# A four-layer pooling and linear-attention trunk: output projection one block later, first attention blocks recorded inside the last pooling unit, loads of x from another queue

## The reference, cut to what matters

```python
h = concat(meta, x)                                  # (8, 16 + 2048, 1024)
for i in range(4):
    j = i // 2
    if i % 2 == 0: h = h + pool_mixer(rmsnorm(h, pool_norm[j]), ...)
    else:          h = h + gla_mixer(rmsnorm(h, gla_norm[j]), ...)
return rmsnorm(h, final_norm)[:, 16:]

def pool_mixer(h, w_in, w_grp, scale, w_out):
    u, z = split(h @ w_in, 2)                        # 2048 channels each, 4 groups of 512
    t[g] = trailing_mean(u[g], window=(2, 4, 8, 16)[g]) - u[g]
    y = einsum(t, w_grp) * scale * silu(z)
    return y @ w_out

def gla_mixer(h, w_in, w_gate2, b_gate, head_norm, w_out):
    q, k, v, z, glr = split(h @ w_in)                # 4 heads, dk 256, dv 512, gate rank 16
    log_a = log_sigmoid(glr @ w_gate2 + b_gate) / 16
    # chunk by chunk: decayed q and k, masked attention within the chunk, carried state S
    o = per_head_rmsnorm(att @ v + qe @ S) * head_norm
    return (o * silu(z)) @ w_out
```

## Time and profile before

| What | Value |
|---|---|
| Median of 3 runs | 1991.08 us (1990.86 to 2058.15) |
| Profiled execution | 2008.14 us; span of its slowest core (3) 2006.5 us |
| Spans of its eight cores | 1978.1 to 2006.5 us |
| PE (TensorE matmul) busy on core 3 | 1907.1 us, 95% of the span |
| VectorE, ScalarE, POOL busy | 66%, 64%, 22% |
| DMA moved | 106.99 MB, mean 53 GB/s |
| Chain that ended last | PE 79%, DVE 5%, issue 5%, POOL 4%, DMA 4%, ACT 3% |

### The profile page before, as it was taken

How to read it: one execution, slowest core, us unless ns; L and a number is a source line. 1 busy time by engine, 2 the same in 40 slices (tenths; PEclk the granted TensorE clock), 3 DMA queues, 4 the chain that set the end, 5 groups by cost and what they waited for, 6 DMA issues and landing times.

```text
span 2006.5 us, 45600 instructions; the slowest of 8 cores (1978.1 to 2006.5 us)
## 1 busy us (share of the span) xinstructions
PE 1907.1 (95%) x16072; PEld 1357.0 (68%) x16072; DVE 1323.1 (66%) x2159; ACT 1293.4 (64%) x2727; POOL 447.6 (22%) x469
## 2 busy tenths in 40 slices
PE   3999999989999999999999999998899999999997
PEld 2767667755666776777676766776667777776774
DVE  1845565765667777777775556467667777777787
ACT  4855445655567666677885545555666766766786
POOL 1747753210000000000015768331100000000000
PEclk8999999987899999999999999999899999999999
DMA  9431212442121212113333212233512212121112
GB/s 186 100 61 33 43 33 43 78 76 59 29 50 30 51 30 45 38 28 58 61 66 60 44 33 36 40 58 74 93 33 38 43 30 51 30 51 31 41 66 83
DMA packets 105152, 106.99 MB, mean 53 GB/s; under 512 B 90192, under 2 KB 92128, under 8 KB 97888
## 3 DMA queue, kind: packets, MB, share of 16 engines
q0 software_dynamic: 11472, 63.53, 18.0%
q1 hardware_dynamic: 91152, 32.17, 7.4%
q10 hardware_dynamic: 2304, 8.39, 1.5%
HBM read 138.22 MB, written 8.39 MB: 73 GB/s over the span
## 4 chain that ended last, share of the span: by engine, by line
PE 79%; DVE 5%; issue 5%; POOL 4%; DMA 4%; ACT 3%; ACTq 0%; DVEq 0%; SPq 0%; POOLq 0%
PE ps L407 79%; DMA hnT<-hnb 3%; POOL SA L446 2%; POOL SB L446 2%; DVE Y L446 1%; DVE hnb L441 1%; DMA gbc<-gains 1%; DMA h<-x 1%; ACT hnb L435 1%; DVE Eq L780 0%; ACT Eq L435 0%; POOL U L451 0%; DVE h L446 0%; ACT sg L435 0%; DVE S L441 0%
## 5 line engine op out<-in xcount | busy, mean ns | idle before, releaser
L407 PE MATMUL ps<-hnT,W 128*128 128x256 bf16 (+1 forms) x9216 | 984.1, 264 | 9.5 <-DVE qe L441 3.6
L407 PEld LDWEIGHTS ps<-hnT,W 128*128 128x128 bf16 x9216 | 832.9, 99 | 155.5 <-issue 19.6
L441 DVE SCALAR_TENSOR_TENSOR h<-ps,rs,h 128x512 f32<-128x512 f32 x256 | 191.4, 748 | 155.5 <-ACT rs L435 130.1
L407 PE MATMUL ps<-W,Y 128*128 128x512 bf16 x1024 | 250.8, 387 | 16.9 <-DVE Y L446 15.1
L407 PE MATMUL ps<-W,hnT 128*128 128x512 bf16 x1088 | 261.7, 385 | 0.0
L446 DVE TENSOR_TENSOR h<-h,ps 128x512 f32<-128x512 f32 x256 | 175.1, 685 | 129.1 <-PE ps L407 126.9
L407 PE MATMUL ps<-W,yT 128*128 128x512 bf16 x1024 | 245.8, 382 | 0.4 <-DVE S L441 0.4
L451 POOL COPY el<-Eq 128x2 f32<-128x2 f32 x136 | 28.2, 208 | 852.6 <-ACT Eq L435 781.3
L446 POOL TENSOR_TENSOR SA<-U 128x1080 f32<-128x1080 f32 (+7 forms) x72 | 140.5, 1952 | 322.5 <-ACT U L435 251.1
L435 ACT ACTIVATE U<-ps,vec 128x256 f32<-128x256 f32 (+2 forms) x288 | 130.0, 451 | 120.7 <-PE ps L407 83.3
L435 ACT ACTIVATE Sb<-S,el 128x512 bf16<-128x512 f32 x256 | 183.8, 718 | 17.2 <-DVE S L441 12.1
(11 more groups left out here) (83 smaller groups left out, 2226.0 us busy)
## 6 DMA issues: line engine op xcount, KB each, us to landing
W<-wpack POOLq DMA_DIRECT2D x55, 1024.0 KB, 8.5
h<-x ACTq DMA_DIRECT2D x16, 512.0 KB, 4.6
out<-h SPq DMA_DIRECT2D x16, 512.0 KB, 2.6
W<-wpack POOLq DMA_DIRECT2D x10, 512.0 KB, 6.9
gbc<-gains SPq DMA_DIRECT2D x5, 512.0 KB, 4.3
kd<-ke SPq DMA_TRANSPOSE x128, 2.3
hnT<-hnb SPq DMA_TRANSPOSE x48, 3.2
Wglr<-wglrp POOLq DMA_DIRECT2D x2, 132.0 KB, 19.3
```

The lines of the kernel that those rows point to most:

```text
L407: ins = e.matmul(o_, lhsT=l_, rhs=r_, start=st, stop=sp_)
L441: P.op("dve", lambda e: e.scalar_tensor_tensor(out=out_, in0=a, scalar=s, in1=b, op0=op0, op1=op1), reads, writes, dve_dur(free_n(out_)) + ...
```

## The change

The output projection of a pooling block is recorded after the next block's window instead of its own (pend). gla_layer no longer records its work at once: it returns an object with gates, start and run. gates(0) is recorded in the last pooling unit, at the head of its last block but one (bi == 7), start (proj_qk(0), turn_k, gates(1)) after the last block's window and ahead of the last outp. glr_block lags three blocks instead of one, and its last three calls move into the first three GLA steps. The last pooling unit uses three projection banks instead of four. plan_pool and plan_gla are laid out anew, so that Eq, Ek and the small tiles cover SB, the first qe, ke, vb cover U0, kd and sz0 cover Y0 and Y1. The loads of x move from ScalarE's to SP's queue and are ordered anew with the constants and the first unit's weights. The planner's DMA constants change; x has no channel of its own in the planner any more.

```diff
-    DMA_NS_PER_BYTE = 1.0 / 200.0
+    DMA_NS_PER_BYTE = 1.0 / 270.0
     DMA_FIX = 2200.0
+    TR_FIX = 5000.0
...
-                o.done = dma_free[o.chan] + self.DMA_FIX
+                o.done = dma_free[o.chan] + (self.DMA_FIX if o.chan == "bulk" else self.TR_FIX)
...
+    plan_pool = [("SB", 4352, ...), ("U0", 4352, ...), ("Y0", 2048, ...),
+                 ("Y1", 2048, ...), ("sg0", 2048, ...), ("sg1", 2048, ...),
+                 ("U1", 4352, ...), ("SA", 4352, ...), ("Y2", 2048, ...), ("ident", 256, ...)]
...
     def pool_layer(li, ui0):
         j = li // 2
-        nproj[0] = 4
-        order = range(4)
-        for gi in order:
+        nxt = gla_layer(li + 1, ui0 + 4) if li + 1 < n_layers else None
+        for gi in range(4):
+            last = gi == 3 and nxt is not None
+            nproj[0] = 3 if last else 4
...
+                if last and bi == NB - 2:
+                    nxt.gates(0)
...
                 window()
-                outp()
-                if gi == 3 and bi > 0 and li + 1 < n_layers:
-                    glr_block(bi - 1, 4)
+                if pend[0] is not None:
+                    pend[0]()
+                pend[0] = outp
+                if last and bi >= 3:
+                    glr_block(bi - 3, 4)
...
+        if nxt is not None:
+            nxt.start()
+        pend[0]()
+        pend[0] = None
+        return nxt
...
-        dma("pool", "wglr", ..., 128 * 8 * 66 * 4)
+        dma("pool", "wglr", ..., 128 * 8 * 66 * 4, after=[P.last_pe])
...
-        nproj[0] = 3
-        gates(0)
-        proj_qk(0)
-        turn_k(0, 0)
-        turn_k(0, 1)
-        gates(1)
+        def start():
+            proj_qk(0)
+            turn_k(0, 0)
+            turn_k(0, 1)
+            gates(1)
...
+                if k_ < 3:
+                    glr_block(NB - 3 + k_, 4)
...
     def xload(i, after=()):
-        return dma("act", "x%d" % i, h[:, i - 1, :], xv[:, i - 1, :], [], [hb[i]], 524288, chan="x", after=after)
+        return dma("sp", "x%d" % i, h[:, i - 1, :], xv[:, i - 1, :], [], [hb[i]], 524288, after=after)
...
+    xs = [xload(1)]
     load_gain(0)
+    dma("sp", "gT", ...)
+    dma("sp", "meta", ...)
     dma("pool", "cst", ...)
+    dma("pool", "Wg", ...)
+    wu = [dma("pool", "Wu%d" % k, ...) for k in range(2)]
+    dma("sp", "vec", ..., after=[xs[0]])
+    dma("sp", "cst3", ..., after=[xs[0]])
+    xs += [xload(i, [xs[0]]) for i in (2, 3)]
+    wz = wload(0, 1, 4096, 8192, Wt[0][1][:], "W01", after=[wu[0]])
+    xs += [xload(i, [wu[1]]) for i in (4, 5)]
+    wload(0, 2, 8192, 12288, Wt[0][2][:], "W02", after=[wz])
     for i in range(6, NT):
         xs.append(xload(i, [xs[i - 3]]))
...
-    for li in range(n_layers):
-        (pool_layer if li % 2 == 0 else gla_layer)(li, 4 * li)
+    for li in range(0, n_layers, 2):
+        nxt = pool_layer(li, 4 * li)
+        if nxt is not None:
+            nxt.run()
```

More of the change, by code:

```diff
@@ L124, in schedule @@
         order = {e: [] for e in ENGS}
-        dma_free = {"bulk": 0.0, "x": 0.0, "tr": 0.0}
+        dma_free = {"bulk": 0.0, "tr": 0.0}
         def release(o):
@@ L365, in build @@
     tens = {}
-    plan_pool = [("SB", 4352, F32, [128, 4, 272]), ("U1", 4352, F32, [128, 4, 272]), ("sg0", 2048, F32, [128, 2, 256]),
-                 ("SA", 4352, F32, [128, 4, 272]), ("sg1", 2048, F32, [128, 2, 256]), ("U0", 4352, F32, [128, 4, 272]),
-                 ("Y0", 2048, BF16, [128, 4, 256]), ("Y1", 2048, BF16, [128, 4, 256]), ("Y2", 2048, BF16, [128, 4, 256]),
+    plan_pool = [("SB", 4352, F32, [128, 4, 272]), ("U0", 4352, F32, [128, 4, 272]), ("Y0", 2048, BF16, [128, 4, 256]),
+                 ("Y1", 2048, BF16, [128, 4, 256]), ("sg0", 2048, F32, [128, 2, 256]), ("sg1", 2048, F32, [128, 2, 256]),
+                 ("U1", 4352, F32, [128, 4, 272]), ("SA", 4352, F32, [128, 4, 272]), ("Y2", 2048, BF16, [128, 4, 256]),
                  ("ident", 256, BF16, [128, 128])]
@@ L371, in build @@
                 ("el0", 32, F32, [128, 2, 2]), ("el1", 32, F32, [128, 2, 2]), ("el2", 32, F32, [128, 2, 2]), ("el3", 32, F32, [128, 2, 2]),
+                ("rs0", 32, F32, [128, 1]), ("rs1", 32, F32, [128, 1]), ("gap", 64, F32, [128, 16]),
                 ("qe0", 1024, BF16, [128, 2, 256]), ("ke0", 1024, BF16, [128, 2, 2, 128]),
-                ("vb0", 1024, BF16, [128, 512]), ("vb1", 1024, BF16, [128, 512]),
+                ("vb0", 1024, BF16, [128, 512]), ("vb1", 1024, BF16, [128, 512]), ("am0", 256, BF16, [128, 128]),
+                ("kd0", 512, BF16, [128, 256]), ("kd1", 512, BF16, [128, 256]), ("kd2", 512, BF16, [128, 256]),
+                ("am1", 256, BF16, [128, 128]),
+                ("sz0", 2048, BF16, [128, 4, 256]),
                 ("gs0", 2048, F32, [128, 2, 256]), ("gs1", 2048, F32, [128, 2, 256]),
[L375 to L378, removed]
+                ("qe1", 1024, BF16, [128, 2, 256]), ("ke1", 1024, BF16, [128, 2, 2, 128]), ("vb2", 1024, BF16, [128, 512]),
                 ("sz1", 2048, BF16, [128, 4, 256]),
-                ("kd1", 512, BF16, [128, 256]), ("kd2", 512, BF16, [128, 256]), ("am1", 256, BF16, [128, 128]),
                 ("S", 4096, F32, [128, 2, 512]), ("Sb", 2048, BF16, [128, 2, 512]),
                 ("o2", 1024, BF16, [128, 4, 128]),
-                ("yT0", 1024, BF16, [128, 4, 128]), ("yT1", 1024, BF16, [128, 4, 128]),
-                ("rs0", 32, F32, [128, 1]), ("rs1", 32, F32, [128, 1])]
+                ("yT0", 1024, BF16, [128, 4, 128]), ("yT1", 1024, BF16, [128, 4, 128])]
     A = {}
@@ L459, in build @@
     b_iw = b_m16 = Buf("iw")
-    dma("sp", "cst3", invw[:], cst[:, 256:328], [], [b_iw], 32768)
-    dma("sp", "vec", vec[:], vecp[:, :], [], [b_vec], 40960)
-    dma("sp", "gT", gT[:], gainT[:, :], [], [b_gT], 20480)
     b_ones, b_eps, b_nb = Buf("ones"), Buf("eps"), Buf("nb")
@@ L465, in build @@
     P.op("dve", lambda e: e.memset(epsc[:], EPS), [], [b_eps], 100.0)
-    P.op("dve", lambda e: e.tensor_scalar(out=nbias[:], in0=vec[:, 64:80], scalar1=-1.0, scalar2=None, op0=ALU.mult),
-         [b_vec], [b_nb], 100.0)
     pscale = lambda j, c: vec[:, 16 * j + c:16 * j + c + 1]
@@ L477, in build @@
     wg_at = {}
+    pend = [None]
     b_wuh = [Buf("wu0"), Buf("wu1")]
[L480 to L491, removed]
     def load_piece(ui, b, last_op):
@@ L701, in window, with outp @@
                     tt("dve", [A[fin], A[Yn]], [A[Yn]], Y[:, :, 0:n], F[:, :, 16:e_], Y[:, :, 0:n], ALU.mult)
-                def outp():
+                def outp(gi=gi, Yn=Yn, Y=Y, Wo=Wo, s=s, tiles=tiles, c0=c0):
                     for t_ in tiles:
@@ L741, in pool_layer @@
                     load_gain(min(li + 1, 4))
+        if nxt is not None:
[3 more added lines that the diff above has]
+        return nxt
     def gla_consts(j):
-        dma("pool", "wglr", Wglr[:, :, :], wglrp[j].rearrange("p (kc n) -> p kc n", kc=8), [], [b_wglr], 128 * 8 * 66 * 4)
+        dma("pool", "wglr", Wglr[:, :, :], wglrp[j].rearrange("p (kc n) -> p kc n", kc=8), [], [b_wglr], 128 * 8 * 66 * 4, after=[P.last_pe])
         for hd in range(2):
@@ L749, in load_wg2 @@
         k = hd % 2
-        dma("pool", "wg2%d" % k, wg2[:, k * 256:(k + 1) * 256], wg2p[j][:, hd * 256:(hd + 1) * 256], [], [b_wg2[k]], 66 * 1024)
+        dma("pool", "wg2%d" % k, wg2[:, k * 256:(k + 1) * 256], wg2p[j][:, hd * 256:(hd + 1) * 256], [], [b_wg2[k]], 66 * 1024, after=[P.last_pe])
+    class GlaLayer:
+        pass
     def gla_layer(li, ui0):
@@ L952, in build, with run @@
-    load_gain(0)
-    dma("pool", "cst", T["ident"][:], cst[:, 0:128], [], [A["ident"]], 65536)
-    dma("sp", "meta", hmf, metaT[:, :], [], [hb[0]], 65536)
+        def start():
[3 more added lines that the diff above has]
+            gates(1)
+        def run():
+            nproj[0] = 3
+            for k_, (hd, bi) in enumerate(steps):
+                ui = ui0 + hd
+                load_piece(ui + 1, bi, [P.last_pe])
+                proj_vz(k_)
+                if k_ < 3:
+                    glr_block(NB - 3 + k_, 4)
+                if k_ + 1 < len(steps):
+                    proj_qk(k_ + 1)
+                    turn_k(k_ + 1, 0)
+                if k_ + 2 < len(steps):
+                    gates(k_ + 2)
+                for k, (t_, o, m) in enumerate(offs_of(bi)):
+                    chunk(k_, k, t_, o, m)
+                    if k == 0 and k_ + 1 < len(steps):
+                        turn_k(k_ + 1, 1)
+                if bi == 4 and ui + 1 < len(units) and units[ui + 1][0] % 2 == 0:
+                    fold(ui + 1)
+                if hd == 0 and bi == NB - 1:
+                    load_gain(min(li + 1, 4))
+                if bi == NB - 1 and hd < 2:
+                    load_wg2(j, hd + 2)
@@ L955, in build @@
+        g = GlaLayer()
+        g.gates, g.start, g.run = gates, start, run
+        return g
     xv = x.rearrange("p (t d) -> p t d", t=16)
     def xload(i, after=()):
```

(29 more changed lines are left out.)

## The result

The changed kernel takes 1938.81 us against 1991.48 in the same comparison: ratio 0.9735, 95% interval [0.9713, 0.9757]. It is faster by 52.7 us where 46 were forecast (1945), and inside the range. On another chip it took 1937.75 against 2011.39: 0.9638 [0.9619, 0.9657]. Ratios, means and the run times of the experiments leave out executions in which a die ran disturbed, and a mean is over the spans of the cores of those that are left, without cores granted under 0.984 of the clock.

What follows compares the result with a forecast made beforehand. PE is busy throughout the GLA layer, leaving its waits in the opening, for Y and in the passages. 12 + 13 + 21 + 8 - 6 - 2 = 46 us off 1991.1 gave 1945 us; own range 1930 to 1960, eight in ten 1920 to 1974.

Steps and rivals of the forecast that it cites:

- Opening, 12 taken: Start of the kernel: reordered loads let projections begin near 30 us instead of 45; gain 12 us, bounds 4 and 17.
- W02's issue: Opening: W02 waits for W01, landing at 41 to 42 us, 3 us later than now, wanted by the lagged outp(0).
- it would come 3 us sooner: Opening: with one queue row fewer the weights get half instead of a third early on, so Wu0 lands some 3 us sooner.
- Y, 13 taken: Pooling units: outp one block later removes 13 of the 18.4 us of waits for Y; bounds 5 and 18.
- 10 us of slack: Window-16 unit: outp one block later has 10 us of slack against a deficit of 0.5 us a block, 4 in the unit.
- the lag moves the wait: Rival for the pooling units: POOL's pace binds through the U buffers, 5 of 18 us gained; 1953 us, chance 0.10.
- Passages, 21 and 8 taken: Two passages from pooling to GLA: 21 of 26.7 us of waits go, and 8 of 12 us at half clock rate.
- Planner's prices, 0 taken: Planner's new 5 us for transposes: little order hangs on it within GLA; 0 us, bounds -3 and +3.
- Banks, 6 taken: Last pooling unit: three projection banks instead of four cost 6 us; bounds 0 and 34.
- my step by U0: Passages: qe0, ke0 lie on U0, free once block 8 has copied its head; part of the 21 us taken.
- Banks give it back: Rival: banks and ScalarE make the last unit and first GLA steps lose some 20 us in two layers; 1965 us, chance 0.20.
- 540 x 0.19: Rival: the lower clock holds for a whole GLA layer of 540 us, costing 101 us; 2046 us, chance 0.03.

## Why the prediction was right, step by step

**The sum** was 46; by medians and means the gain is 51 to 53, inside the range. That core 1 of the two profiles differs by 46.1 is luck. Errors cancel in the sum: the opening and Y were given 25 us and their stretches brought 17, the two passages were given 29 less 8 of costs and theirs brought 36.

**Opening, 12 taken: 4 to 8.** ScalarE's stand for x went as said, and the first projection came 12 us earlier (medians of eight cores, 44.7 and 32.7), of which about half lasts; where the other half goes no run shows. One step of the working failed. W02's issue was to follow W01's landing at once; W01 landed at 34.1 (23.1 + 11.0), but the planner had put the issue behind POOL's first window, at 42.5. PE stood 0.3 us for it in the end, with the lagged outp behind other work. For Wu0, put at 19.7, one core is no measure: the median is 20.5, and 19.5 before. By the rule of the Trainium skill ("DMA: Bandwidth & Descriptors", Queues, rings and completion order) I had said that it would come 3 us sooner. Wg, ahead of it on the same queue, did come sooner (12.6 after 14.7, medians), Wu0 did not, so the traces do not bear that use of the rule out.

**Y, 13 taken: 2.6 of the waits.** Two things lie in this number. The lag alone takes 8.6 us of them on core 1 (18.5 to 9.9), and the three banks put back 5.8 (15.8, and 10.0 with four). The step that failed is that 10 us of slack would cover the window-16 unit: in the two of them 13.1 us of waits for Y (core 3 before) became 7.6 (core 4 after). Its rival, that the lag moves the wait, is right there (an outp still waits 2.1 us, POOL's period is 10.96 as before), though not by the U buffers as I had it but by the one SB. Yet the lag is a large part of the change, 23 us alone and 32 on top of the rest. I had looked for its worth where the waits for Y stood and not in the passages, where without it PE loses 16.3 us instead of 2.9 in the first.

**Passages, 21 and 8 taken: some 34.** Idle time and lost clock of 38 us (13.1 + 13.0 + 7 + 5) went to under 4. The reason given, that glr_block asks later and finds its transpose, is only part of it: the planner's prices alone, and the lag alone, each bring the wait for hnT from 15.9 to some 3.5 us on core 1 and end those for Eq and qe.

**Planner's prices, 0 taken: 25 alone.** Mis-sized most. I had looked for its effect within GLA, on kd, and found none; the transposes that PE had waited for were hnT's. Singly, prices and lag give 25 and 23 and take largely the same waits in the passages. The opening and the early step cost 5.5 and 7.5 when undone. But all the rest of the change without the lag is worth 20, less than the prices alone, so other parts lean on the lag. No part has a value of its own, and no run has just the prices and the lag.

**Banks, 6 taken: 7. Layout:** my step by U0 was not needed.

**Rivals.** Neither of the two profiles of the changed kernel has a stage at 0.81 on any of its eight cores; what brings that stage on stays open (last section). Its price, 540 x 0.19, is 103 and not 101. "Banks give it back" was the right mechanism at a third of its price.

## What to carry to other kernels

Before pricing a new order, ask which later work it leaves at hand for the engine that binds; a lag pays where that work fills somebody else's wait, not only where its own wait stood. A list planner's durations are part of the kernel: two of them were worth 25 us without an instruction changed. Compare each with the trace, and with its slow cases rather than its median, since an engine that runs in a fixed order stands for the slow ones. And price parts of a change against each other, not only against the kernel before: the prices alone gave 25 us, and with all other parts but the lag beside them 20. Compare kernels over all cores: one core of one execution was 6 us off here.

## What the runs showed of the hardware that I had not expected

**How long a transpose takes.** In the profile of the kernel before, all eight cores together, 230 hnT transposes ran with no weight load (W, Wglr, wg) in flight on their core and took 3.0 to 4.9 us from issue to landing. Of the 154 with one in flight 113 took more than 5 us, the longest 11.1. So the planner's one price can fit only one of the two kinds.

**The stage at 0.81.** In that profile cores 2 and 3 have it, from 416 us to 578 but for one short grant of 0.5, and 4 to 8 us behind a grant of 0.5 in the passage; cores 0 and 1, on the same die and as busy, do not (length, busy PE and the others, clock; core 1, then core 3):

```profile
480.00:570.00 90.00, 90.00 (x738) 62.15 (x737) 64.49 (x120) 61.20 (x124) 3.98 (x14) 1.00 0.22 42
480.00:570.00 90.00, 90.00 (x655) 59.64 (x653) 53.79 (x98) 54.89 (x107) 2.91 (x12) 0.81 0.16 30
```

It is no chance of one execution. On the chip of the last experiments the median of the kernel before was 2011.4 us, and in each of the four executions that its ratio uses one or two neighbouring pairs of cores had 0.971 to 0.975 of the clock and 2000 to 2010 us, the others 1978 to 1989. The changed kernel's cores stood there between 1927.6 and 1936.1, all at 0.994 or more. It would be easy to conclude that the pause in the passage brings the stage on, but other runs speak against it. On the chip of the first experiments the kernel before, which pauses there, had no core under 0.984 in the seven executions that count, while the changed kernel with the old opening, which has no grant of 0.5 in either passage of its profile, had a pair at 0.979 and 0.980 in one of three. None of these executions has a trace but its mean clock; that the pairs had the same stage is inferred. The cause is not known.

**POOL beside VectorE.** The head copy of U, of 64 columns, took 0.23 us on POOL alone and 1.23 beside VectorE's product into Y, ending 0.09 us after it (229.35 + 1.23 and 228.08 + 2.41, core 4 of the changed kernel).
